# A value projection of two token halves made in Strassen's seven-product form, with its operand sums on GpSimd

## What is computed

```python
m = x @ w_in
q, k, v, xr, gr, gates = jnp.split(m, cuts, axis=-1)
...
v = v.reshape(B, S, ATTN_HEADS, 2 * HEAD_DIM)
ya = diff_attention(q, k, v, lambda_qk, subln_g, lam_init)
```

## Time and profile before

| | |
|---|---|
| median of 3 runs | 3474.32 us (3473.58 to 3478.85) |
| profiled execution, first to last instruction | 3468.5 us |
| TensorE matmul busy | 3163.5 us, 91% |
| VectorE busy | 2265.4 us, 65% |
| ScalarE busy | 723.2 us, 21% |
| GpSimd busy | 594.6 us, 17% |
| mean granted TensorE clock | 0.961 |

### The profile page before, as it was taken

One profiled execution on the slowest core, in us unless ns is written; L12 is line 12 of the kernel. 1 busy time (PEld: TensorE's weight loads), 2 busy tenths in 40 slices (PEclk: granted clock), 3 DMA queues, 4 the chain that ended last, 5 costly groups with the idle time before them and its releaser, 6 DMA issues. The chain is left out here.

```text
span 3468.5 us, 55454 instructions
## 1 busy us (share of the span) xinstructions
PE 3163.5 (91%) x20794; PEld 2387.7 (69%) x20794; DVE 2265.4 (65%) x5755; ACT 723.2 (21%) x1783; POOL 594.6 (17%) x516
## 2 busy tenths in 40 slices
PE   8999889999999999999998988887899989888877
PEld 8996579999968979997885434343578864444433
DVE  8844648778576548772457777776634467777775
ACT  2101311111131211111322222222212322222222
POOL 0000000000000000000004544444100035444442
PEclk9999699999999989999999999999999999999998
DMA  5443014455312014452449999999734479999998
GB/s 203 161 161 121 1 67 163 160 174 183 134 61 87 4 63 170 162 218 85 158 164 407 421 422 422 422 421 421 303 124 158 194 288 421 421 422 422 422 421 330
DMA packets 116014, 829.18 MB, mean 239 GB/s; under 512 B 12784, under 2 KB 14320, under 8 KB 17424
## 3 DMA queue, kind: packets, MB, share of 16 engines
q0 software_dynamic: 73728, 536.90, 37.3%
q1 hardware_dynamic: 39488, 273.59, 21.3%
q10 hardware_dynamic: 2576, 15.59, 1.2%
HBM read 824.99 MB, written 1.05 MB: 238 GB/s over the span
## 5 line engine op out<-in xcount | busy, mean ns | idle before, releaser
L3194 PE MATMUL psum_all<-expert_rows,const_sb 128*128 128x512 f32 x2048 | 963.6, 628 | 189.0 <-ACT const_sb L3109 188.8
L2782 POOL DMA_INDIRECT expert_rows<-in_peer_uv_dram,head_experts x512 | 594.4, 1161 | 2831.1 <-issue 1911.2
L3194 PEld LDWEIGHTS psum_all<-expert_rows,const_sb 128*128 128x128 f32 x2048 | 403.1, 201 | 731.8 <-issue 465.9
L2934 DVE CUSTOM_DVE_ANT_0 expert_rows<-expert_rows,xn 128x1024 f32<-128x1024 f32 x512 | 616.5, 1223 | 256.3 <-DMA expert_rows<-in_peer_uv_dram,head_experts 252.3
L2457 PE MATMUL psum_all<-x,weight_ring 128*128 128x256 f32 x1024 | 228.6, 381 | 0.0
L3109 ACT ACTIVATE const_sb<-cst,head_weights 128x128 f32<-128x128 f32 x496 | 158.6, 390 | 329.4 <-DVE head_weights L2945 326.0
L409 PE MATMUL psum_all<-xn,weight_ring 128*128 128x136 f32 (+1 forms) x1408 | 193.1, 281 | 20.6 <-DMA weight_ring<-in_ffn_in_dram 9.6
L2457 PEld LDWEIGHTS psum_all<-x,weight_ring 128*128 128x128 f32 x1024 | 192.3, 191 | 28.2 <-issue 3.5
L409 PEld LDWEIGHTS psum_all<-xn,weight_ring 128*128 128x128 f32 x1408 | 176.7, 193 | 22.1 <-issue 9.8
L409 PE MATMUL psum_all<-xn,weight_sums 128*128 128x136 f32 (+1 forms) x1056 | 142.6, 278 | 0.6 <-DVEq L641 0.6
L3105 ACT ACTIVATE dots<-dots 128x4 f32<-128x4 f32 x124 | 25.5, 205 | 559.5 <-DVE dots L2934 559.4
(11 more groups left out here) (617 smaller groups left out, 5099.5 us busy)
## 6 DMA issues: line engine op xcount, KB each, us to landing
weight_ring<-in_ffn_in_dram SPq DMA_DIRECT2D x88, 1024.0 KB, 4.8
weight_ring<-in_w_in_dram SPq DMA_DIRECT2D x48, 1024.0 KB, 4.8
weight_ring<-in_ffn_out_dram SPq DMA_DIRECT2D x32, 1024.0 KB, 4.8
weight_ring<-in_ffn_out_dram SPq DMA_DIRECT2D x16, 768.0 KB, 4.2
weight_ring<-in_hyb_in_dram SPq DMA_DIRECT2D x12, 1024.0 KB, 4.8
weight_ring<-in_peer_q_dram SPq DMA_DIRECT2D x12, 1024.0 KB, 15.6
expert_rows<-in_w_v_dram ACTq DMA_DIRECT2D x8, 1024.0 KB, 5.9
weight_ring<-in_br_attn_dram SPq DMA_DIRECT2D x8, 1024.0 KB, 7.0
```

Source lines behind the costliest of these rows:

```text
L2782: pool.indirect_dma_start(out=rows[:, j, :], out_offset=None, in_=a["peer_uv"], in_offset=bass.IndirectOffsetOnAxis(ap=idx[:, n, j:j + 1], ...
L2934: dve.tensor_tensor_reduce(row, row, xt[:, n, :], 1.0, 0.0, ALU.mult, ALU.add, dots[:, n, j:j + 1]).then_inc(S.dotted, 1)
L3194: mm = pe.matmul(sums(n, half), diag[:, j, :], rows[:, j, D + half * 512:D + (half + 1) * 512], start=False, stop=last and j == TOPK - 1)
```

## The change

The value projection of both layers takes the same seven-product form. The 2x2 blocks are the two token halves, the even and odd width groups, and two sets of columns: within each 512 columns of v the first 256 and the second 256 (index f). Each of the seven products is four matmuls of 512 columns (two runs of 256). The four sums of weight blocks (`v_sums`, 128x2048 each) are made on GpSimd once all four DMAs of the v weights have landed. In layer 0 GpSimd also makes the four sums of token blocks (`h_sums`, 128x512 each) once `h` is complete; in layer 1 the sums made for the query and key (`tin`) serve. The v weights are now loaded in steps 0 to 3. The products go to psum[0..3], so that TensorE waits for step 6's `take`, no more for step 7's. ScalarE copies products 1 and 2 and the first finished quarter; VectorE makes the two middle sums and three quarters of `v`. A memset of the padding columns of 48 tiles of `z`, early in the phase, goes, and one of 8 tiles comes behind the sixth product (`v_sums` lies where the others stand).

```diff
+QUARTER = D // 4
+v_sums = arena[:, NQK * (PADC + T2):NQK * (PADC + T2) + 4 * KP * 2 * QUARTER].rearrange("p (s j g m) -> p s j g m", s=4, j=KP, g=2)
+v_part = wsum.rearrange("p b s j m -> p (b s j m)")[:, 0:4 * 2 * QUARTER].rearrange("p (q g m) -> p q g m", q=4, g=2)
+v_raw = wv.rearrange("p (j e) (g f m) -> p j e g f m", e=2, g=2, f=2)
+h_pairs = h.rearrange("p (j e) t -> p j e t", e=2)
+h_sums = tin if l else area(cuts[1], 4, KP, HALF)
+v_bank = [psum[i][:, :].rearrange("p (g m) -> p g m", g=2) for i in range(4)]
+v_out = lambda n, f: v[:, n, :].rearrange("p (g f m) -> p g f m", g=2, f=2)[:, :, f, :]
...
-            if p % 2 == 0:
-                act.dma_start(wv[:, p:p + 2, :], a["w_v2"][l][:, p:p + 2, :]).then_inc(S.v_weights, 16)
+            if p < KP:
+                act.dma_start(wv[:, 2 * p:2 * p + 2, :], a["w_v2"][l][:, 2 * p:2 * p + 2, :]).then_inc(S.v_weights, 16)
...
+        act.wait_ge(S.v_products, 1)
+        act.activation(v_part[:, P1], v_bank[0], ACT.Copy).then_inc(S.v_copied, 1)
+        act.wait_ge(S.v_products, 2)
+        act.activation(v_part[:, P5], v_bank[1], ACT.Copy).then_inc(S.v_copied, 1)
+        act.wait_ge(S.v_products, 5)
+        act.activation(v_out(0, 0), v_bank[0], ACT.Copy).then_inc(S.v_copied, 1)
+        act.wait_ge(S.v_copied, 3)
...
-        pe.wait_ge(S.taken, 3 * QK)
-        pe.wait_ge(S.v_weights, 16 * KD // 2)
+        def v_product(out, left, right, onto=False):
+
+            for j in range(KP):
+                mm = pe.matmul(out, left(j), right(j), start=j == 0 and not onto, stop=j == KP - 1, skip_group_check=onto)
+            mm.then_inc(S.v_products, 1)
+
+        pe.wait_ge(S.taken, 3 * (QK - 1))
+        pe.wait_ge(S.fourth, QK - 1)
+        pe.wait_ge(S.v_weights, 16 * KP)
         if l == 0:
             pe.wait_ge(S.h_ready, KD)
-        for n in range(QT):
-            for half in range(2):
-                for k in range(KD):
-                    mm = pe.matmul(psum[4 + 2 * n + half][:, :], h[:, k, n * P:(n + 1) * P], wv[:, k, half * 512:(half + 1) * 512],
-                                   start=(k == 0), stop=(k == KD - 1))
-                mm.then_inc(S.v_ready, 1)
+        v_product(v_bank[0], lambda j: h_pairs[:, j, 0, lo], lambda j: v_raw[:, j, 0, :, 0, :])
+        pe.wait_ge(S.v_sums, 1)
+        if l == 0:
+            pe.wait_ge(S.v_inputs, 1)
+        v_product(v_bank[1], lambda j: h_sums[:, 0, j, :], lambda j: v_sums[:, 0, j])
+        pe.wait_ge(S.v_sums, 2)
+        if l == 0:
+            pe.wait_ge(S.v_inputs, 2)
+        v_product(v_bank[2], lambda j: h_sums[:, 1, j, :], lambda j: v_sums[:, 1, j])
+        pe.wait_ge(S.v_sums, 3)
+        if l == 0:
+            pe.wait_ge(S.v_inputs, 3)
+        v_product(v_bank[3], lambda j: h_sums[:, 2, j, :], lambda j: v_sums[:, 2, j])
+        pe.wait_ge(S.v_copied, 1)
+        v_product(v_bank[0], lambda j: h_pairs[:, j, 1, lo], lambda j: v_raw[:, j, 1, :, 0, :], onto=True)
+        pe.wait_ge(S.v_copied, 2)
+        pe.wait_ge(S.v_sums, 4)
+        v_product(v_bank[1], lambda j: h_pairs[:, j, 1, hi], lambda j: v_sums[:, 3, j], onto=True)
+        pe.wait_ge(S.v_third, 1)
+        if l == 0:
+            pe.wait_ge(S.v_inputs, 4)
+        v_product(v_bank[3], lambda j: h_sums[:, 3, j, :], lambda j: v_raw[:, j, 1, :, 1, :], onto=True)
...
+    @block.gpsimd
+    def _(pool):
+        pool.wait_ge(S.v_weights, 16 * KP)
+        pool.tensor_tensor(v_sums[:, 0], v_raw[:, :, 0, :, 1, :], v_raw[:, :, 1, :, 1, :], ALU.add).then_inc(S.v_sums, 1)
+        pool.wait_ge(S.v_sums, 1)
+        pool.tensor_tensor(v_sums[:, 1], v_sums[:, 0], v_raw[:, :, 0, :, 0, :], ALU.subtract).then_inc(S.v_sums, 1)
+        pool.tensor_tensor(v_sums[:, 2], v_raw[:, :, 0, :, 0, :], v_raw[:, :, 0, :, 1, :], ALU.subtract).then_inc(S.v_sums, 1)
+        pool.wait_ge(S.v_sums, 2)
+        pool.tensor_tensor(v_sums[:, 3], v_raw[:, :, 1, :, 0, :], v_sums[:, 1], ALU.subtract).then_inc(S.v_sums, 1)
+        pool.wait_ge(S.v_sums, 4)
+        if l == 0:
+            pool.wait_ge(S.h_ready, KD)
+            pool.tensor_tensor(h_sums[:, 0], h_pairs[:, :, 0, hi], h_pairs[:, :, 0, lo], ALU.subtract).then_inc(S.v_inputs, 1)
+            pool.wait_ge(S.v_inputs, 1)
+            pool.tensor_tensor(h_sums[:, 1], h_pairs[:, :, 1, hi], h_sums[:, 0], ALU.subtract).then_inc(S.v_inputs, 1)
+            pool.tensor_tensor(h_sums[:, 2], h_pairs[:, :, 1, hi], h_pairs[:, :, 0, hi], ALU.subtract).then_inc(S.v_inputs, 1)
+            pool.wait_ge(S.v_inputs, 2)
+            pool.tensor_tensor(h_sums[:, 3], h_pairs[:, :, 1, lo], h_sums[:, 1], ALU.subtract).then_inc(S.v_inputs, 1)
+            pool.wait_ge(S.v_inputs, 4)
...
-        step(dve.memset(z[:, :, 0:PADC], 0.0))
...
-        for n in range(QT):
-            for half in range(2):
-                dve.wait_ge(S.v_ready, 2 * n + half + 1)
-                last = dve.tensor_copy(v[:, n, half * 512:(half + 1) * 512], psum[4 + 2 * n + half][:, :])
-        step(last)
+        dve.wait_ge(S.v_products, 3)
+        dve.wait_ge(S.v_copied, 1)
+        dve.tensor_tensor(v_part[:, U2], v_part[:, P1], v_bank[2], ALU.add).then_inc(S.v_second, 1)
+        dve.wait_ge(S.v_products, 4)
+        dve.wait_ge(S.v_second, 1)
+        dve.tensor_tensor(v_part[:, U3], v_part[:, U2], v_bank[3], ALU.add).then_inc(S.v_third, 1)
+        dve.wait_ge(S.v_third, 1)
+        dve.wait_ge(S.v_copied, 2)
+        step(dve.tensor_tensor(v_out(1, 1), v_part[:, U3], v_part[:, P5], ALU.add))
+        dve.wait_ge(S.v_products, 6)
+        step(dve.tensor_tensor(v_out(1, 0), v_part[:, U2], v_bank[1], ALU.add))
+        step(dve.memset(z[:, NQK:NQK + KD, 0:PADC], 0.0))
+        dve.wait_ge(S.v_products, 7)
+        step(dve.tensor_tensor(v_out(0, 1), v_part[:, U2], v_bank[3], ALU.add))
```

More of the change, by code:

```diff
@@ L2230, in second_block @@
                     quad = lambda p: [psum[4 * (p % 2) + i][:, 0:HALF] for i in range(4)]
-                    with phase(nc, "extra", "products", "weight_sums", "input_sums", "copied", "second", "third", "fourth", "taken", "scaled_out", "vectors", "v_weights", "v_ready", "soft_exp", "soft_log", "lam_sums", "lam_exp",
+                    QUARTER = D // 4
[6 more added lines that the diff above has]
+                    v_out = lambda n, f: v[:, n, :].rearrange("p (g f m) -> p g f m", g=2, f=2)[:, :, f, :]
+                    with phase(nc, "v_sums", "v_inputs", "v_products", "v_copied", "v_second", "v_third", "extra", "products", "weight_sums", "input_sums", "copied", "second", "third", "fourth", "taken", "scaled_out", "vectors", "v_weights", "soft_exp", "soft_log", "lam_sums", "lam_exp",
                                "constants", "root", "h_ready", shared=w.landed[0]) as (block, S):
```

## The result

The changed kernel takes 3494.2 us, the median of five runs, against 3478.85 us for the kernel before in five runs of the same comparison. The ratio is 1.0063, with a 95% interval of 1.0046 to 1.0079. The prediction was 3492 us and a slower kernel. Single runs of either kernel spread over some 10 us and more (before: 3467 to 3484 us over all comparisons), so the places are compared by the two phases of the trace. Each run's time lies 1.7 to 2.1 us above its own span; the 6 us named ahead of the result is not a fixed difference, but comes from a profiled execution (3468.5 us) that was one of the short ones.

A forecast was written before the change was run, and what follows sets the result against it. TensorE alone was taken to set the time in these phases. Losses of 8.2 + 11.2 + 2.5 + 4.0 = 25.9 us less 8.0 us gained gave +17.9 us on 3474.3 us: 3492 us, range 3465 to 3503 us.

The forecast's parts named there:

- the 6 us named ahead of the result: Whole program: the profiled span of 3468.5 us was put about 6 us below the runs, the same difference for either kernel.
- The gain: Value stage, both layers: fewer matmuls 7.0 us, wait before v 0.8 us, layer 0 memset 0.2 us; together -8.0 us.
- The loads at nothing: Steps 0 to 3: issuing v weight loads sooner costs nothing; 5.9 us to landing, then GpSimd can begin.
- The hold: Steps 3 to 6: VectorE instructions with two SBUF inputs wait while GpSimd reads SBUF; chance 0.55, time 3481 to 3503 us.
- GpSimd's price g: One GpSimd weight sum of 128x2048: taken as 3.6 us, between 2.4 and 14 us from VectorE rows.
- The stalls: Product 7 of step 5 waits for VectorE's third part: 8.2 us late in layer 1, 11.2 us in layer 0.
- my formula: Third part of step 5 ready at 2516.1 + 4g (layer 1) and 1541.7 + 4g (layer 0), against 2522.3 and 1544.95 us.
- The token sums: Layer 0, step 6: four GpSimd sums of 0.9 us hold VectorE again, 3.6 less the lead of 1.1: 2.5 us lost.
- The clock: After each of two stalls TensorE runs 4 us of matmuls at clock 0.50, losing 2.0 us each, 4.0 us together.
- The sum: Both phases: 8.2 + 11.2 + 2.5 + 4.0 = 25.9 us lost, 8.0 us gained, so +17.9 us.

The follow-up runs named there:

- e1: The changed kernel without GpSimd's sums, products taking raw blocks, v not computed: 3465.03 us against 3474.29 us for the kernel before, ratio 0.9975.
- e7: The kernel before with only the v weight loads moved to steps 0 to 3: phases 82.2 and 82.4 us, against 82.1 and 81.9 us.
- e2: The changed kernel with GpSimd writing a constant (memset) in place of its eight sums, v not computed: phases 77.9 and 78.3 us.
- e3: The changed kernel with GpSimd copying one block in place of each of its eight sums, v not computed: phases 83.2 and 80.1 us.
- e6: The changed kernel with GpSimd's same eight sums started only once step 6 is taken: phases 87.6 and 80.5 us.
- e8: The changed kernel run again without edit, the second comparison: 3497.95 us against 3473.38 us for the kernel before, ratio 1.0069.
- e4: The changed kernel with each GpSimd weight sum cut into four of 128x512: phases 93.0 and 80.7 us, against 94.2 and 93.4 us uncut.

## Why the prediction was right, point by point

- **The gain** was put at 8.0 us; e1 measures 7.8 us. The count of matmuls, the wait of 0.38 us that goes and the last VectorE instruction of 0.69 us all stand.
- **The loads at nothing**: right (e7). GpSimd began 30.1 us after the start of the phase in layer 0 and 31.0 us in layer 1, where the forecast has 29.2 and 29.0 us: the loads take 6.9 us to land in the median, not 5.9, and up to 8.7. (This execution came to the phase of layer 0 at 1499.9 us, before at 1505.8, so the clock times of the two traces differ.)
- **The hold** as the mechanism, with one VectorE instruction let in between two of GpSimd's: right in each row, and shown by e1, e2 and e3. The rule of the Trainium skill, SBUF — State Buffer, "Who interferes with whom", agrees with the trace: weight sums of 4.80 us against 0.69.
- **GpSimd's price g** was the term that was too small: 3.6 us were taken, 4.5 to 5.0 measured (the four weight sums of layer 0 start 4.87, 4.81 and 4.92 us apart). The Trainium skill, GPSIMD Engine Reference, "Performance versus the Vector engine", gives 4497 ns; the shortest in e6 is 4493 ns. My rows bounded it only between 2.4 and 14 us, and I chose low. With this term alone put at 4.5 us the sum of the prediction comes to +26 us.
- **The stalls.** Layer 1: forecast 8.2, measured 12.3 us. Layer 0: forecast 11.2 in step 5, measured 2.86 us in step 4 and 10.63 us more in step 5, together 13.5 us. At g = 4.8 my formula gives 13.0 and 16.0 us, at g = 4.5 it gives 11.8 and 14.8. The first is too long in both layers, since it counts the instructions let in between as time of their own, 1.5 and 1.8 us, while GpSimd's sums start 4.87, 4.81 and 4.92 us apart with these instructions already in that.
- **The token sums** were put at 2.5 us and cost TensorE nothing: they hold weight sums for 1.4 to 1.7 us each, but TensorE was itself behind by then, at the lower clock, and no wait follows. This term was wrong, and its error stood against the one in g.
- **The clock** was put at 2.0 us for each long stall; measured 2.4 us in layer 0 and 2.5 us in layer 1.
- **The sum**: +17.9 us forecast for the phases, +23.6 us measured (+21.7 us in e8); the medians differ by 15.4 us in the first comparison and 24.6 us in the second. The direction came from the mechanism; that the first median lies 2 us from the forecast is in part luck, since the price of GpSimd's sums was too low by a fifth, the token sums were too dear, and the median of a comparison moves by several us with the rest of the program.

## What to carry to other kernels

Before work is moved to GpSimd, look at what VectorE does in those microseconds: while GpSimd reads SBUF, each VectorE instruction with two SBUF inputs waits for the end of GpSimd's, so long GpSimd instructions cost VectorE their full length, and TensorE too where it stands close behind VectorE. Ask first whether the busy engine has free time a few microseconds later; here the 25.6 us of GpSimd work in layer 0 were some 12 us of VectorE's (four of 2.28 and four of 0.69 us), and they fitted where it waited for TensorE anyway. If GpSimd must do it, only what writes without reading was free here (e2). Shorter instructions let VectorE through more often, which gave back 12.7 us in layer 1 and 1.2 in layer 0 (e4). Work placed where VectorE mostly reads PSUM cost less, but a short chain of eight columns was enough to spoil it (e6).

## What the runs showed of the hardware that was not expected

- In e6 a VectorE instruction with one SBUF input was held as well: TENSOR_SCALAR on 128x8, 4.37 us for 0.17. RECIPROCAL, also with one input, ran its usual 0.20 us at 1572.22, in the middle of a GpSimd token sum of 1.26 us that began at 1572.12; the addition of two SBUF tiles behind it was held (0.95 us). The Trainium skill, SBUF — State Buffer, "Who interferes with whom", counts `tensor_scalar` among the instructions that can take the shared pair of ports. That eight columns are enough was not clear to me.
- The time that VectorE is held stands in its own busy time, with no idle ahead of it. The page alone reads as if VectorE had more to do: 49.5 to 69.0 us in layer 0.
- It goes both ways. In e4 GpSimd's pieces of 128x512 have 1.26 us at least and 1.71 us in the median, where VectorE's weight sums stand between them. In the changed kernel the long sums that start beside the end of a held weight sum of 128x512 take 4.85 to 4.96 us, and those that start beside the end of L2421, of 128 columns, take 4.54 us. That GpSimd waits there for VectorE's instruction is how I read it.
